# Expert stage of a fused decoder kernel: two items interleaved, results scattered item by item into PSUM

## What is computed

```python
def hierarchical_moe(h, w_router_group, w_router_expert, w_gate, w_up, w_down):
    ...
    comb = (one_hot(g_idx, G)[:, :, None] * exp_w[:, None, :] * g_gate[:, None, None])
    y = zeros_like(h)
    for g in range(G):
        hg = einsum('td,edf->tef', h, w_gate[g])
        hu = einsum('td,edf->tef', h, w_up[g])
        act = silu(hg) * hu * comb[:, g, :, None]
        y = y + einsum('tef,efd->td', act, w_down[g])
    return y
```

## Time and profile before

| what | value |
| --- | --- |
| median of three runs | 1577.62 us |
| profiled execution, span from first to last instruction | 1575.9 us |
| what lies around the span, against the median | 1.7 us |
| PE busy in the span | 1412.2 us (90%) |
| DVE busy | 891.4 us (57%) |
| ACT busy | 613.8 us (39%) |
| read from HBM | 393.83 MB |
| mean granted TensorE clock | 0.967 of full |
| expert transfers of 2 MB | 96 |

### The profile page before, as it was taken

One profiled execution on the slowest core, in us unless ns is written; L12 is line 12 of the kernel. 1 busy time (PEld: TensorE's weight loads), 2 busy tenths in 40 slices (PEclk: granted clock), 3 DMA queues, 4 the chain that ended last, 5 costly groups with the idle time before them and its releaser, 6 DMA issues.

```text
span 1575.9 us, 25855 instructions
## 1 busy us (share of the span) xinstructions
PE 1412.2 (90%) x10318; PEld 1117.4 (71%) x10318; DVE 891.4 (57%) x1227; ACT 613.8 (39%) x817; POOL 33.0 (2%) x69
## 2 busy tenths in 40 slices
PE   8999999999999999999999999999886666666666
PEld 7888888888888888877788888778653434333333
DVE  5777688577776777765457776777621121121121
ACT  6443465563445543466654344664211001000000
POOL 4000000000000000000010000010000000000000
PEclk9999999999999999999999999999999889989889
DMA  7565543456565555554456556557999999999996
GB/s 239 198 209 191 188 160 134 134 169 218 172 209 164 188 196 197 167 177 142 134 150 214 196 166 211 161 171 271 396 400 427 428 428 428 430 428 429 428 428 291
DMA packets 149044, 396.67 MB, mean 252 GB/s; under 512 B 8003, under 2 KB 106387, under 8 KB 136704
## 3 DMA queue, kind: packets, MB, share of 16 engines
q1 hardware_dynamic: 147424, 392.20, 66.9%
q0 software_dynamic: 1440, 3.72, 1.0%
q10 hardware_dynamic: 128, 0.03, 0.0%
HBM read 393.83 MB, written 1.05 MB: 251 GB/s over the span
## 4 chain that ended last, share of the span: by engine, by line
PE 75%; DMA 19%; DVE 4%; ACT 2%; issue 1%; SPq 0%; ACTq 0%; DVEq 0%; POOL 0%; POOLq 0%
DMA pair_ring<-in_w_exp_up 19%; PE psum L557 17%; PE psum L258 12%; PE psum L260 12%; PE psum L259 12%; PE psum L563 9%; PE psum L2342 6%; PE psum L1024 1%; DVE low L253 1%; PE psum L2369 1%; PE psum L1435 1%; DVE hT L445 1%; ACT hT L435 0%; PE psum L2380 0%; PE psum L424 0%
## 5 line engine op out<-in xcount | busy, mean ns | idle before, releaser
L253 DVE TENSOR_TENSOR low<-raw,high 128x2048 fp32r<-128x2048 f32 x179 | 409.6, 2291 | 193.6 <-ACT high L249 193.1
L249 ACT ACTIVATE high<-raw 128x2048 fp32r<-128x2048 f32 x179 | 341.2, 1910 | 125.1 <-PE psum L563 90.2
L557 PE MATMUL psum<-hT,high 128*128 128x512 f32 x1152 | 288.0, 392 | 0.1
L557 PEld LDWEIGHTS psum<-hT,high 128*128 128x128 f32 x1152 | 209.3, 189 | 39.3 <-DVE low L253 0.4
L2342 PE MATMUL psum<-pair_ring,gain 128*32 128x256 f32 x1984 | 140.2, 445 | 96.1 <-DMA pair_ring<-in_w_exp_up 96.1
L258 PE MATMUL psum<-high,hT 128*128 128x512 f32 x496 | 200.1, 403 | 6.9 <-DVE low L253 4.5
L260 PE MATMUL psum<-high,hT 128*128 128x512 f32 x496 | 194.5, 392 | 0.0
L259 PE MATMUL psum<-low,hT 128*128 128x512 f32 x496 | 193.9, 391 | 0.0
L2342 PEld LDWEIGHTS psum<-pair_ring,gain 128*32 128x32 f32 x1984 | 77.4, 128 | 158.4 <-issue 134.6
L563 PEld LDWEIGHTS psum<-hT,low 128*128 128x128 f32 x1152 | 157.1, 190 | 11.2
L563 PE MATMUL psum<-hT,low 128*128 128x256 f32 x1152 | 160.6, 282 | 0.0
(11 more groups left out here) (356 smaller groups left out, 1452.5 us busy)
## 6 DMA issues: line engine op xcount, KB each, us to landing
pair_ring<-in_w_exp_gate SPq DMA_DIRECT2D x31, 2048.0 KB, 18.9
pair_ring<-in_w_exp_up SPq DMA_DIRECT2D x31, 2048.0 KB, 23.3
pair_ring<-in_w_exp_down SPq DMA_DIRECT2D x31, 2048.0 KB, 24.4
raw<-in_ffn_w_gate SPq DMA_DIRECT2D x88, 512.0 KB, 4.0
raw<-in_ffn_w_up SPq DMA_DIRECT2D x88, 512.0 KB, 5.0
raw<-in_ffn_w_down SPq DMA_DIRECT2D x88, 512.0 KB, 4.3
raw<-in_gla_w_in SPq DMA_DIRECT2D x24, 512.0 KB, 4.5
raw<-in_sb_w_in SPq DMA_DIRECT2D x24, 512.0 KB, 4.7
```

Source lines behind the costliest of these rows:

```text
L249: act.activation(high[:, p % RING, :], raw_of(p), ACT.Copy).then_inc(rounded, 1)
L253: dve.tensor_tensor(low[:, p % RING, :], raw_of(p), high[:, p % RING, :].bitcast(F32), ALU.subtract).then_inc(split, 1)
L557: pe.matmul(to.rearrange("p (o n) -> p o n", o=2), w_high, both_parts, start=kk == 0, stop=False, skip_group_check=True)
```

## The change

- **Order on PE.** The gate and up products of item j+1 come ahead of the transposition and the down product of item j. For that, items alternate between two PSUM banks (`ITEM_BANK`) and two copies of the small buffers in SBUF.
- **Scatter per item.** `scatter` multiplies one item's result at once. The result stays as four quarters on 32-row strips, as `down` leaves it, so the eight products use 32 rows each (`spread` now holds the shares four times, once per strip). They run in two groups of four, with a wait of PE on itself between the groups, so that two strips don't write one bank. They add to `SUM_Y`, four PSUM banks that the kernel fills with x at the start (four products with the identity, in place of fourteen that only kept PE busy), and that ACT and DVE copy to SBUF once, at the very end. The scatter of an item stands one item later in PE's order; that of a batch's last item stands in the next batch, or behind the loop.
- **One copy of the down result.** ACT alone copies it, 128 partitions x 256 (`result`).
- **Ten fixed slots.** Item j's gate and up always go to the same place, and down matrices alternate between two places. One of these, `early_pair`, is new memory that no earlier layer uses; its first transfer is issued between the mixer's two groups of weights. The new order of the loads is gate and up of item j, then down of item j-1.
- **Events.** `pair_used` now counts one per `gate_up` and one per `down`, eight a batch; `BOTH_AT` and `DOWN_AT` say which count belongs to which.
- **Routing.** The sum over shares on DVE is 1024 wide instead of 256. The multiplication of item 0 (`first_inner`) is placed inside the routing chain. `RANKS` moves to another bank, and PE waits for its copy (`counted`) behind the first `gate_up`. The buffer for descriptors of GpSimd's own queue is set to 4096 bytes, to make room.

The core of the diff:

```diff
+        BATCH_X = [banks(0), banks(1)]
+        SPREAD = banks(0)
+        ITEM_Y = banks(1)[:, 0:2 * P]
+        SUM_Y = [banks(2, 2), banks(4, 2)]
+        ITEM_BANK = [banks(7), banks(6)]
         QUARTER = D // TILES
-        PER_BATCH = 3 * TILES
+        EVENTS = 2 * TILES
+        BOTH_AT, DOWN_AT = [1, 2, 4, 6], [3, 5, 7, 8]
...
-            step(dve.tensor_copy(counts, RANKS))
+            dve.tensor_copy(counts, RANKS).then_inc(e["counted"], 1)
+            dve.wait_ge(e["counted"], 1)
...
             step(dve.scalar_tensor_tensor(item, tile_no, 0.0, item, ALU.is_gt, ALU.mult))
             step(dve.tensor_tensor(by_tile(item), by_tile(item), per_tile(iota[:, 0:EXPERTS]), ALU.add))
             at_choice(item, item_of)
+            first_inner()
             at_choice(place_in, place_of)
...
             first_products(pe, 8, products)
-            hold_clock(pe, 14)
+            for tt in range(TT):
+                for c in range(2):
+                    wait_x(pe, 8, tt, c)
+                    pe.matmul(SUM_Y[tt][:, c * BANK:(c + 1) * BANK], ident[:, :], x[:, tt, c * BANK:(c + 1) * BANK],
+                              start=True, stop=False, skip_group_check=True)
...
         def moe_sp(sp):
 
             sp.wait_ge(h_ready, H_AT["mix"] + 1)
-            for i in (PAIRS + 1, PAIRS + 2):
-                pair_load(sp, i, 0, i // 3)
+            up_load(sp, 0, 0)
+            down_load(sp, 1, 1)
             sp.wait_ge(h_ready, H_AT["n8"])
-            pair_load(sp, PAIRS, 0, PAIRS // 3)
-            for i in range(PAIRS):
-                if i == 1:
-                    sp.wait_ge(split, MOE)
-                elif i == 3:
-                    sp.wait_ge(used, MOE)
-                pair_load(sp, i, 0, i // 3)
-            for i in range(PAIRS + EXTRA, PER_BATCH):
-                sp.wait_ge(pair_used, i - PAIRS - EXTRA + 1)
-                pair_load(sp, i, 0, i // 3)
+            gate_load(sp, 0, 0)
+            gate_load(sp, 1, 1)
+            sp.wait_ge(split, MOE)
+            up_load(sp, 1, 1)
+            gate_load(sp, 2, 2)
+            sp.wait_ge(used, MOE)
+            up_load(sp, 2, 2)
+            gate_load(sp, 3, 3)
+            up_load(sp, 3, 3)
+            for j in (2, 3):
+                sp.wait_ge(pair_used, DOWN_AT[j - 2])
+                down_load(sp, j, j)
             n = last_batch(sp)
-
-            def item_loads(i, c):
-                expert = sp.value_load(plan[0:1, bass.ds(c * TILES + (1 + TILES + i), 1)], min_val=0, max_val=EXPERTS - 1)
-                for j in range(3):
-                    b = (c, 1)
-                    first_reuse = isinstance(c, int) and 3 * i + j < EXTRA
-                    sp.wait_ge(pair_used, at(b, PER_BATCH, 3 * i + j - PAIRS - (EXTRA if first_reuse else 0) + 1))
-                    pair_load(sp, 3 * i + j, b, expert)
-            for i in range(TILES):
-                item_loads(i, 0)
-            with sp.Fori(1, n) as c:
-                for i in range(TILES):
-                    item_loads(i, c)
-            return n
+            with sp.Fori(0, n) as c:
+                b = (c, 1)
+
+                def expert_of(j):
+                    return sp.value_load(plan[0:1, bass.ds(c * TILES + (1 + TILES + j), 1)], min_val=0, max_val=EXPERTS - 1)
+
+                def both(j):
+                    expert = expert_of(j)
+                    sp.wait_ge(pair_used, at(earlier(b), EVENTS, BOTH_AT[j]))
+                    gate_load(sp, j, expert)
+                    up_load(sp, j, expert)
+
+                def down(j):
+                    expert = expert_of(j)
+                    if j < 2:
+                        sp.wait_ge(pair_used, at(earlier(b), EVENTS, DOWN_AT[j + 2]))
+                    else:
+                        sp.wait_ge(pair_used, at(b, EVENTS, DOWN_AT[j - 2]))
+                    down_load(sp, j, expert)
+
+                both(0)
+                for j in range(1, TILES):
+                    both(j)
+                    down(j - 1)
+                down(TILES - 1)
...
+            def scatter(j, b, last=False):
+
+                def one(q, tt):
+                    rows = slice(q * SLOTS, (q + 1) * SLOTS)
+                    return pe.matmul(SUM_Y[tt][:, q * QUARTER:(q + 1) * QUARTER], spread[rows, j, tt * P:(tt + 1) * P],
+                                     item_y[j % 2][rows, :], start=False, stop=False, skip_group_check=True)
+
+                pe.wait_ge(e["y_sb"], at(b, TILES, j + 1))
+                pe.wait_ge(e["shares_sb"], at(b, 2, j // 2 + 1))
+                for q in range(TILES):
+                    ins = one(q, q % 2)
+                ins.then_inc(e["half_scattered"], 1)
+                pe.wait_ge(e["half_scattered"], at(b, TILES, j + 1))
+                for q in (1, 0, 3, 2):
+                    ins = one(q, 1 - q % 2)
+                ins.then_inc(e["all_scattered"] if last else e["scattered"], 1)
...
+                gate_up(0, b)
+                if b == 0:
+                    pe.wait_ge(e["counted"], 1)
+                else:
+                    scatter(TILES - 1, earlier(b))
+                gate_up(1, b)
+                turn_inner(0, b)
+                down(0, b)
+                spread_shares(0, b)
+                gate_up(2, b)
+                scatter(0, b)
+                turn_inner(1, b)
+                down(1, b)
+                spread_shares(1, b)
+                gate_up(3, b)
+                scatter(1, b)
+                turn_inner(2, b)
+                down(2, b)
+                pe.wait_ge(e["shares_sb"], at(b, 2, 2))
+                turn_half(0, following)
+                scatter(2, b)
+                turn_half(1, following)
+                turn_inner(3, b)
+                down(3, b)
 
...
             batch(0, 1)
             n = last_batch(pe)
             with pe.Fori(0, n) as c:
                 batch((c, 1), (c, 2))
+            scatter(TILES - 1, (n, 0), True)
...
+            def silu(j, b):
+                act.wait_ge(pair_used, at(b, EVENTS, BOTH_AT[j]))
+                act.activation(item_gate[j % 2], ITEM_BANK[j % 2][:, P:2 * P], ACT.Silu).then_inc(e["silu"], 1)
+
+            def result(j, b):
+                act.wait_ge(pair_used, at(b, EVENTS, DOWN_AT[j]))
+                if b != 0 or j >= 2:
+                    act.wait_ge(e["scattered"], at(b, TILES, j - 1))
+                act.activation(item_y[j % 2], ITEM_Y, ACT.Copy).then_inc(e["y_sb"], 1)
+
+            def batch(b, following):
+                silu(0, b)
+                for j in range(1, TILES):
+                    silu(j, b)
+                    result(j - 1, b)
                 for half in range(2):
...
+            def batch(b, next_picks):
+                if b != 0:
+                    inner(0, b)
+                inner_turned(0, b)
+                inner(1, b)
+                spread_in(0, b)
+                inner_turned(1, b)
+                inner(2, b)
+                spread_in(1, b)
+                picks_of(dve, next_picks)
+                inner_turned(2, b)
+                inner(3, b)
+                inner_turned(3, b)
+
+            route_dve(dve, step, lambda: inner(0, 0))
+            batch(0, 1)
             n = last_batch(dve)
...
+            dve.wait_ge(e["all_scattered"], 1)
+            for c in range(2):
+                dve.tensor_copy(x[:, 1, c * BANK:(c + 1) * BANK], SUM_Y[1][:, c * BANK:(c + 1) * BANK]).then_inc(e["copied_dve"], 1)
...
             in_loads(sp, "mix_in")
+            down_load(sp, 0, 0)
             out_loads(sp, "mix_out")
-            n = moe_sp(sp)
-            for tt in range(TT):
-                for j in range(2):
-                    c = slice(j * BANK, (j + 1) * BANK)
-                    sp.wait_ge(e["added"], n * 2 * TT + (2 * tt + j + 1))
+            moe_sp(sp)
+            for j in range(2):
+                c = slice(j * BANK, (j + 1) * BANK)
+                for tt, copied in ((0, e["copied_act"]), (1, e["copied_dve"])):
+                    sp.wait_ge(copied, j + 1)
                     sp.dma_start(out[0, tt * P:(tt + 1) * P, c], x[:, tt, c]).then_inc(stored_out, 16)
```

254 lines of the change are left out of this document (100 added, 154 removed).

## The result

The changed kernel takes **1586.22 us** (median of 4 runs, 1583.56 to 1586.66) against 1577.9 us for the kernel before in runs beside it (4 runs, 1577.44 to 1582.16). The ratio is 1.0046, with a 95% interval of 1.0032 to 1.0060: slower by half a per cent. The forecast was 1584.0 us, range 1575 to 1590.

The account below looks back on a forecast made before the run. The prediction took the expert stage as bound by its stream of loads. Last up matrix 0.9 us earlier and end chain 7.3 longer gave +6.4, span 1582.3; with 1.7 from profiled span to median, 1584.0 us, range 1575 to 1590.

Parts of the forecast that it names:

- The first reuse: Expert stage's start: tenth and eleventh transfers wait for down of items 0 and 1; pauses 10.3 and 4.2 us.
- the reuse comes in time: Rival: down of item 0 ends before the stream runs dry, early transfer counts in full, 1575.1 us; chance 0.12.
- The early transfer: One matrix loaded behind the mixer's last input weights, worth -4.9 us of stream.
- The loop doesn't starve: In the loop, the tightest reuse, down of item 3, has 7 us of slack; effect zero.
- Wider sums, first products: Routing's wider sum over shares and the products that load x fall into existing waits; effect zero.
- Last up matrix: Last up matrix of the stream lands at 1557.5, 0.9 us earlier than before.
- The end: From the last up matrix to the span's end, PE's chain takes 24.8 us against 17.5, 7.3 longer.
- The last gate/up product: First product behind the last up matrix: 5.33 us, starting at a clock of 0.50 after idleness.
- Strips don't overlap: Rival: scatters take 3.7 us, 2.4 more, three times at the end and once before the eleventh transfer: 1593.6; chance 0.07.
- The drain: Rival: six more switches of PE's array form at the end cost 1.8 us in all, 1585.8; chance 0.12.
- A shorter end: Rival: clock still up before the last gate_up (-1.7), scatters save 1.2, second pause 1 us shorter: 1580.1; chance 0.12.
- The loop starves: Rival: loads in the loop come 2 us short per pass, 14 us in all: 1598; chance 0.03.

Follow-up runs that it names:

- Experiment 2: Changed kernel with gate and up of the second batch's first two items loaded ahead of the waiting down matrices: 1574.92 us, ratio 0.9969.
- Experiment 1: Changed kernel with item 0's down matrix loaded behind the mixer again, not ahead of its output weights: 1586.52 us, ratio 1.0036.
- experiment 12: As experiment 10, but item 0's down matrix is loaded at the head of the expert stage, not among the mixer's weights: 1567.42 us, ratio 0.9918.
- experiment 4: Changed kernel with eight identity products ahead of gate/up of item 3 in each batch: 1584.52 us, ratio 1.0029.
- experiment 6: The changed kernel once more, unedited, on another chip: 1586.51 us, ratio 1.0046.
- experiment 3: Changed kernel with the last batch written out without the gathering for a batch that never comes: 1583.73 us, ratio 1.0027.
- experiment 9: Changed kernel, last batch written out, item 1's scatter and item 2's turning ahead of the last gate/up, item 3's turning before item 2's scatter: 1580.79 us, ratio 1.0010.
- experiment 10: Changed kernel with the edits of Experiment 2 and experiment 9 together: 1568.31 us, ratio 0.9933.
- experiment 11: As experiment 10, with six identity products ahead of the last gate/up product: 1569.37 us, ratio 0.9940.

## Why the prediction was right, and where its steps were off

- **The stream bounds the stage: right.** 429 GB/s from 1200 to 1540, against 428 before.
- **The first reuse: right to 0.2 us.** The forecast, from the first issue, had the tenth transfer at 55.7 and the eleventh at 64.9; they came at 55.5 and 64.9. The reason holds too: DVE's route ends at 1134.25, PE has waited 1.64 us for the copy behind it. Experiment 2 shows that these two waits are the pauses and cost 12 us. With that the rival *the reuse comes in time* fell: it wanted `down` to end at 1129, and it ended at 1136.4.
- **The early transfer, "worth -4.9 us of stream": right in the sum, wrong by itself.** Experiment 1 put its worth in this kernel at nothing. The sum stayed right because it went from the time at which the stream runs dry, counted the early matrix among those already through, and so used the one and the longer pause together. That it would be worth 4.9 us where the pause is gone, which the first rival assumed, fell with experiment 12: 1.8 by its profile, nothing by its median.
- **The loop doesn't starve: right.** No pause in the stretches, and 2 us more of PE's work for each batch in experiment 4 changed nothing.
- **Wider sums, first products: right.** Neither has an effect: DVE still waits 1.25 us for silu behind the wider sum, and the first `gate_up` begins 43.9 us behind the first issue in both kernels.
- **Last up matrix: forecast 0.9 us earlier against the start of the stage, measured 1.7.** The rate was 429, not 428 GB/s; over 85 matrices that makes 0.9 us (415.6 against 416.5).
- **The end, 24.8 us forecast: measured 25.9.** Each of three scatters took 1.44 us to the next instruction (1.58 the last), not 1.3: together 0.6. The turning of item 3 took 1.49, since PE also waits for ACT's copy of the gathered rows: 0.1. ACT's copy of the last result with its waits 0.65, not 0.45; the last copies and stores 4.98, not 4.72. Against that, the last up matrix was 0.8 us earlier than forecast, so the error of the sum is smaller than those of its parts.
- **The last gate/up product: right in its time, by luck.** The forecast took over 5.33 us from the kernel before, where the granted clock was at 0.50, the lower of its two levels, before the product began (0.50 from 1555 to 1557, the product from 1558.54). Here the idle time ahead of it was 2.47 us, the product began at 1555.91 at the full clock, and the clock fell only while it ran. It took 5.35 us. Stretches of the changed kernel's span:

```profile
1555.00:1557.00 2.00, 1.09 (x20) 0.68 (x24) 1.93 (x5) 0.00 (x0) 0.00 (x0) 1.00 1.01 434
1557.00:1559.00 2.00, 2.00 (x28) 1.03 (x24) 0.81 (x1) 0.00 (x0) 0.00 (x0) 0.55 1.02 434
1559.00:1561.00 2.00, 2.00 (x28) 0.94 (x20) 0.00 (x0) 0.00 (x0) 0.00 (x0) 0.59 1.01 434
```

At the full clock the product takes 3.66 us (experiment 4), and this term would have been 1.7 us too high.

- **Sum: +6.4 forecast, +6.8 by the profiles**, and 1584.0 forecast against 1586.22. The sum missed by 0.4 of these 2.2 us; the rest is no term of it: the changed kernel's stage began at 1080.97 in one profile and at 1083.77 in the other, and the kernel before, in the 18 runs beside the first four experiments, had a median of 1579.76 us (1577.07 to 1583.36), 2.1 above the 1577.62 that the forecast was built on. In the comparisons of experiments 1 and 6 the changed kernel, or the one equal to it, stands 6.8 and 7.4 us above the kernel before (1579.76 and 1579.16).
- **The rivals.** *Strips don't overlap* fell: 1.52 us for sixteen records. *The drain* fell. Its price, 0.29 us a switch, had no row (it is the length of DVE's copy, 0.35 less 0.06), and here each product of another form begins within the last 0.1 us of the one before it (`down`, with columns, ends at 1565.92, the gathering, with the whole array, begins at 1565.85; the scatter, with strips, ends at 1569.36, the gathering begins at 1569.28). The profile models these ends, but the starts alone say the same: 1.86 us from `down` to the gathering and 1.99 from there to the scatter, where the sum had 1.93 and 1.92. The Trainium skill (TensorEngine Tiling (Array Packing), Key Properties) says that a change of the tiling mode drains the engine. If it does here, it costs nothing that these rows show. *A shorter end* didn't come by itself; experiments 3, 4 and 9 brought it, by 2.9, 1.7 and 7.0 us. *The loop starves* fell, as above.
- **Two slips in the prediction**, without effect. Half of the strips' price is half of 4 x 2.4, so 4.8 and not 4.2, and the range would end at 1590.6. And the last of the 40 slices has 291 GB/s: the full rate holds from slice 31 to 39.

So both of the forecast's causes stand: the pauses at the first reuse (12 us), and the work behind the last up matrix (8.4 us more). They are two separate mistakes of order, and mending both makes 1568.3 us, 0.7% below the kernel before. What the new order of the products is worth in the loop stays at nothing, since the stream bounds it.

Where the 12.0 us come from by which experiment 10 is shorter than the kernel before, the same account shows. The stream's end, from the first issue and by the data of the last stretches, is 478.9 us before, 482.0 in the changed kernel, 470.3 in experiment 10 (344, 172 and 33 GB/s from 1552 in steps of 2 us, so 1554.6) and 471.9 in experiment 12. Less the 1.55 us of the first issue and 4.90 for each matrix (96 before and in experiment 12, 95 in the other two), the stream pauses 6.9, 15.0, 3.2 and 0 us in all; the kernel before had more than its two visible pauses of about 2 us. So 8.6 of the 12.0 us are the stream's (7.0 in experiment 12, without the early matrix), and 3.4 are the work behind its end (11.8 us against 15.2). Which parts of the change shorten that work was not taken apart.

## What to carry to other kernels

- In a stage bound by one stream of loads, write down three numbers: when the stream starts, how long it pauses, and how much work is behind its last load. An order of products matters through these alone. A queue that issues in program order pauses for whatever its next entry waits for, so sort the first reuses by when their places become free, not by item.
- Work that is put one item later to keep an engine busy comes out behind the loop. Write the last pass out, keep in it only what is needed, and put ahead of the last wait what needs no more loads. Move a product only together with its transfer.
- A transfer moved to an earlier stage is worth its length less every pause that it would have filled: here nothing with a pause of 10 us behind it, and at most 1.8 of 4.9 us without.

## What I had not expected

- Runs of one kernel differ by 3 us ahead of the stage that is changed: with 6 us at stake, compare profiles from the stage's first instruction.
- The granted clock after a short idle time is not the same in each run. The first `down`, after 1.65 us of idleness, took 1.93 us in some profiles and 3.20 to 3.62 in others; the last gate/up product took 5.18 us after 1.27 us of idleness (experiment 10, granted clock 0.50 from 1548 to 1550) and 3.66 us after 1.50 (experiment 12, granted clock 1.00). Where the idle time was filled in part (experiment 4) or wholly (experiment 11) it took 3.66.
- Sixteen records of 256 columns on strips of 32 rows, in two groups of eight with a wait of PE on itself between them, take 1.44 us to the next instruction. One by one they would be 16 x 0.23 = 3.7, always four at once 0.92. Strips overlap, and nearly all of the rest is the wait between the groups (0.49 us of idleness of the weight loads in the trace).
